# Seven block products instead of eight in one more tile of a hybrid block's output projection, with the weights' sums made by accumulating DMAs

## The reference

```
h     = rmsnorm(x, w_norm_pre)
proj  = h @ w_in                      # 1024 -> 3328 columns: q_a k_a v_a z_a q_r f_r i_r z_r
o_a   = sliding_window_attention(rope(q_a), rope(k_a), v_a, sinks) * silu(z_a)
o_r   = rmsnorm(hgrn2(q_r, f_r, i_r)) * silu(z_r)
y     = concat([o_a, o_r]) @ w_out    # 1024 -> 1024
out   = x + rmsnorm(y, w_norm_post)
```

## Time and profile before

| | |
|---|---|
| median of 3 runs | 865.61 us (865.39 to 866.41) |
| the profiled execution, its own time | 864.57 us |
| its span in the trace | 862.7 us |
| granted TensorE clock, mean | 0.999 |
| TensorE busy | 851.9 us |
| VectorE, ACT, GpSimd busy | 631.9, 519.0, 114.6 us |
| moved by DMA | 211.20 MB, mean 245 GB/s |

### The profile page before, as it was taken

The page is one execution under the profiler, slowest core; times in us unless marked ns, Lnnn a source line. Parts: engine busy times, 40 slices in busy tenths (PEclk is TensorE's granted clock), DMA queues, the critical chain, the costliest instruction groups (busy, mean ns, idle before and its releaser), DMA issues.

```text
span 862.7 us, 12445 instructions
## 1 busy us (share of the span) xinstructions
PE 851.9 (99%) x4428; PEld 700.6 (81%) x4428; DVE 631.9 (73%) x1125; ACT 519.0 (60%) x1033; POOL 114.6 (13%) x84
## 2 busy tenths in 40 slices
PE   8999999999999999999999999999999999999997
PEld 6787788888888778888888878888888887888885
DVE  6878878674656799767747789887775368888846
ACT  7766445763466458567446655865853755576544
POOL 0000013430200000332020000144300000004220
PEclk9999999999999999999999999999999999999999
DMA  8686755748986647464898785445699674444586
GB/s 322 212 325 221 244 205 170 285 147 314 418 342 248 213 145 265 152 210 133 321 382 348 276 330 172 146 151 216 241 374 396 228 273 147 147 147 158 189 326 254
DMA packets 59981, 211.20 MB, mean 245 GB/s; under 512 B 6672, under 2 KB 6928, under 8 KB 59920
## 3 DMA queue, kind: packets, MB, share of 16 engines
q1 hardware_dynamic: 57904, 205.56, 65.3%
q10 hardware_dynamic: 2016, 4.85, 1.4%
HBM read 157.95 MB, written 52.43 MB: 244 GB/s over the span
## 4 chain that ended last, share of the span: by engine, by line
PE 84%; DVE 9%; ACT 4%; issue 3%; DVEq 0%
PE bank L596 55%; PE bank L605 5%; PE turn_b L852 3%; PE score_b L852 3%; PE bank L852 3%; PE score_b L605 3%; PE turn_b L605 3%; PE turn_b L653 2%; DVE kv_tok L1386 2%; PE score_b L629 2%; PE turn_b L706 2%; PE bank L697 1%; PE bank L687 1%; PE turn_b L709 1%; ACT probs_t L951 1%
## 5 line engine op out<-in xcount | busy, mean ns | idle before, releaser
L596 PE MATMUL bank<-h_hi,w_lo 128*128 128x512 f32 x832 | 326.9, 393 | 0.0
L596 PE MATMUL bank<-h_lo,w_hi 128*128 128x512 f32 x832 | 326.3, 392 | 0.0
L596 PE MATMUL bank<-h_hi,w_hi 128*128 128x512 f32 x832 | 324.4, 391 | 0.5 <-issue 0.5
L596 PEld LDWEIGHTS bank<-h_lo,w_hi 128*128 128x128 f32 x832 | 156.4, 188 | 34.7 <-issue 3.3
L596 PEld LDWEIGHTS bank<-h_hi,w_hi 128*128 128x128 f32 x832 | 156.4, 188 | 33.1 <-issue 1.0
L596 PEld LDWEIGHTS bank<-h_hi,w_lo 128*128 128x128 f32 x832 | 156.3, 188 | 32.8
L1716 POOL TENSOR_TENSOR mix_lo<-v_r,mix_hi 128x512 fp32r<-128x512 f32 x16 | 21.2, 1322 | 539.0 <-ACT v_r L1142 539.0
L1263 DVE TENSOR_TENSOR w_lo<-w_raw,w_hi 128x1024 fp32r<-128x1024 f32 x36 | 44.8, 1248 | 34.6 <-ACT w_hi L924 34.1
L1386 DVE STREAM_TRANSPOSE kv_tok<-k_mid 32x128 f32<-32x128 f32 x192 | 58.1, 303 | 2.8
L924 ACT ACTIVATE w_hi<-w_raw 128x1024 fp32r<-128x1024 f32 x38 | 39.8, 1051 | 24.9 <-issue 10.2
L1700 POOL TENSOR_TENSOR x_acc<-x_acc,x_sq 128x512 f32<-128x512 f32 x21 | 32.7, 1557 | 70.0 <-ACT x_sq L974 70.0
(11 more groups left out here) (280 smaller groups left out, 1549.2 us busy)
## 6 DMA issues: line engine op xcount, KB each, us to landing
w_hi<-kept_hi SPq DMA_DIRECT2D x108, 512.0 KB, 3.8
w_lo<-kept_lo SPq DMA_DIRECT2D x108, 512.0 KB, 4.9
w_raw<-in_weights SPq DMA_DIRECT2D x46, 512.0 KB, 6.2
kept_hi<-w_hi SPq DMA_DIRECT2D x34, 512.0 KB, 6.3
kept_lo<-w_lo SPq DMA_DIRECT2D x34, 512.0 KB, 7.4
x_in<-in_x_rows SPq DMA_DIRECT2D x8, 1024.0 KB, 8.1
x_in<-in_x SPq DMA_DIRECT2D x15, 512.0 KB, 6.6
kept_lo<-w_raw SPq DMA_DIRECT2D x8, 512.0 KB, 7.0
```

Of the source, the lines that this page charges most:

```text
L596: mm = pe.matmul(acc(w)[:, :], stationary[:, s, k, :], moving[:, k, :], start=(m == 0), stop=(m == 3 * KT - 1), skip_group_check=True)
```

## The change

FAST goes from 2 to 1: tile 1's output projection takes the form of seven block products too. LATE goes from 6 to 2: in tile 1 only weight tiles 0 and 1 are loaded raw and split; 2 to 5 are loaded from the kept parts, which are saved four positions earlier in tile 0 than before.

The sums of weight blocks are no longer made by VectorE. GpSimd issues eight DMAs of 1 MiB in tile 0, from the seventh split on: a block is copied in DRAM to `t_rows`, and another is added to it by an accumulating DMA. There are six phases with a wait between them. The signs of two sums turn, so VectorE negates in `sum_head` and `post`. SP loads the eight sums (512 KiB each): two at tile 0's weight tile 26, two at the start of tile 1 (into the attention's buffers `probs` and `probs_t`), four at its weight tile 4 (into `w_raw`). ACT and VectorE split them in tile 1's steps 1 to 5 (`sum_high`, `sum_low`; the high parts go to `mix_hi` and `mix_lo`), and SP saves them at tile 1's weight tiles 6, 7, 8, 9, 11, 13, 15 and 17. VectorE's first softmax of tile 1 waits until those in the attention's buffers are saved (`probs_saved`).

```diff
+LATE = 2
-FAST = 2
+FAST = 1
-SUMS_IN = (FAST - 1, H0 + 8), (FAST, 5)
-SUMS_OUT = ((FAST, 0, 0), (FAST, 1, 2)), ((FAST, H0, 0), (FAST, H0 + 2, 2))
-SUMS_AT = 5
+SUMS_IN = {(FAST - 1, OUT0): (0, 1), (FAST, 0): (2, 3), (FAST, LATE + 2): (4, 5, 6, 7)}
+SUMS_SPLIT = {1: (0,), 2: (1, 2), 3: (3, 4), 4: (5, 6), 5: (7,)}
+SUMS_OUT = {6: 0, 7: 1, 8: 2, 9: 3, 11: 4, 13: 5, 15: 6, 17: 7}
-LATE = 6
...
+            def load_sum(k):
+                if k == 0:
+                    sp.wait_ge(t_made, 64)
+                if k == 2:
+                    sp.wait_ge(weighed.sem, weighed.after(FAST - 1, PAIRS - 1))
+                    sp.wait_ge(head_mixed.sem, head_mixed.after(FAST - 1, HEADS - 1))
+                if k >= 4:
+                    sp.wait_ge(lo_split.sem, lo_split.after(0, 0) + FRESH - RAW_SLOTS + k - 4)
+                sp.dma_start(t_in[k], t_rows[k * P:(k + 1) * P, :].rearrange("p (k m) -> p k m", k=KT)).then_inc(t_loaded[k], 16)
+            def save_sum(k):
+                sp.wait_ge(t_low, k + 1)
+                rows, saved = slice((WT + k) * P, (WT + k + 1) * P), probs_saved if k in (2, 3) else t_saved
+                sp.dma_start(kept[0][rows, :].rearrange("p (k m) -> p k m", k=2), t_hi[k].bitcast(FP32)).then_inc(saved, 16)
+                sp.dma_start(kept[1][rows, :].rearrange("p (k m) -> p k m", k=KT), t_in[k]).then_inc(saved, 16)
...
-                    if i == FRESH + 1:
-                        for late in range(FRESH + 1 - RAW_SLOTS, FRESH):
-                            save_split(late)
+                    if i == FRESH:
+                        save_split(FRESH - 3)
+                    for k in SUMS_IN.get((t, w), ()):
+                        load_sum(k)
                     if i >= FRESH:
                         load_split(t, w)
+                    if i == FRESH + 1:
+                        for late in (FRESH - 2, FRESH - 1):
+                            save_split(late)
+                    if t == FAST and w in SUMS_OUT:
+                        save_sum(SUMS_OUT[w])
...
+            def sum_high(k):
+                act.wait_ge(t_loaded[k], 16)
+                act.activation(t_hi[k], t_in[k].rearrange("p k m -> p (k m)").rearrange("p (k n) -> p k n", k=2), ACT.Copy).then_inc(t_high, 1)
...
+                            if t == FAST and head == 0:
+                                act.wait_ge(probs_saved, 64)
                             act.activation(o_sq_hi, out_b, ACT.Square)
...
                 dve.wait_ge(turned.sem, turned.after(t, q - 1))
+                if t == FAST and q == 0:
+                    dve.wait_ge(probs_saved, 64)
...
-                dve.tensor_tensor(s_tmp[:, S2, :], h_mix[:, 2 * P:], s3[:, h, :], ALU.subtract).then_inc(s_step, 1)
+                dve.scalar_tensor_tensor(s_tmp[:, S2, :], h_mix[:, 2 * P:], -1.0, s3[:, h, :], ALU.mult, ALU.subtract).then_inc(s_step, 1)
...
+            def sum_low(k):
+                dve.wait_ge(t_high, k + 1)
+                dve.tensor_tensor(t_in[k], t_in[k], t_hi[k].rearrange("p k n -> p (k n)").rearrange("p (k m) -> p k m", m=P), ALU.subtract).then_inc(t_low, 1)
...
-            pool.wait_ge(lo_split.sem, lo_split.after(0, 3))
+            pool.wait_ge(lo_split.sem, lo_split.after(0, 6))
+            def sum_start(dst, src):
+                pool.dma_start(t_rows[dst * 2 * P:(dst + 1) * 2 * P, :], src).then_inc(t_base, 16)
+            def sum_add(dst, src):
+                pool.dma_start(t_rows[dst * 2 * P:(dst + 1) * 2 * P, :], src, accum_op=ALU.add, max_dma_last_dim=4 * KT * P).then_inc(t_made, 16)
+            def block_rows(w):
+                return weights[w * P:(w + 2) * P, :]
+            sum_start(0, block_rows(B11))
+            sum_start(1, block_rows(B22))
+            pool.wait_ge(t_base, 32)
+            sum_add(0, block_rows(B12))
+            sum_add(1, block_rows(B12))
+            pool.wait_ge(t_made, 32)
+            sum_start(2, t_rows[2 * P:4 * P, :])
+            pool.wait_ge(t_base, 48)
+            sum_add(2, block_rows(B11))
+            pool.wait_ge(t_made, 48)
+            sum_start(3, t_rows[4 * P:6 * P, :])
+            pool.wait_ge(t_base, 64)
+            sum_add(3, block_rows(B21))
```

More of the change, by code:

```diff
@@ L68 @@
 FAST_WT = OUT0 + len(FAST_ROWS)
-SPLIT_SLOT += [w % 4 for w in range(WT)] + [(WT + w) % 4 for w in range(FAST_WT)] * (TILES - FAST)
-assert WT == 34 and OUT0 == 26 and FAST_WT % 4 == 0 and FAST == 2
+SPLIT_SLOT += [w % 4 for w in range(FAST_WT)] * (TILES - FAST)
+assert WT == 34 and OUT0 == 26 and FAST_WT % 4 == 0 and FAST == 1
 UNITS = [(w, k, i) for w, ks in ((P1A, (0, 1)), (P1B, (2, 3)), (P7A, (0, 1)), (P7B, (2, 3)), (P2A, (0, 1)), (P6A, (0, 1)), (P4A, (0, 1)))
@@ L187, in after, with hybrid_block @@
         return self.per_tile + (sum(self.sizes[:tile]) if tile >= 0 else tile * self.per_tile) + i + 1
-def hybrid_block(nc, x, x_rows, weights, cos, sin, vectors, w_post, squares, out, kept):
+def hybrid_block(nc, x, x_rows, weights, cos, sin, vectors, w_post, squares, out, kept, t_rows):
     ctx = ExitStack()
@@ L270, in hybrid_block @@
         u4 = [probs[:, 4 * i:4 * i + 4, :].rearrange("p b n -> p (b n)") for i in range(2)]
-        t_hi = [t_more[:, 0, :, :], t_probs[:, 1, :, :], t_more[:, 1, :, :], t_probs[:, 0, :, :]], \
-               [mix[:, 2 * i:2 * i + 2, :] for mix in (mix_hi, mix_lo) for i in range(2)]
+        t_in = [area[:, i, :, :] for area, n in ((t_more, 2), (t_probs, 2), (w_raw, RAW_SLOTS)) for i in range(n)]
+        t_hi = [mix[:, 2 * i:2 * i + 2, :] for i in (2, 3, 1, 0) for mix in (mix_hi, mix_lo)]
         y_stats = sb("y_stats", [16])
@@ L343, in hybrid_block @@
         a_sum, y_kept, y_took, y_posted = (Count(sem(n), i, 0) for n, i in (("a_sum", 1), ("y_kept", 6), ("y_took", 8), ("y_posted", 8)))
[L344 removed]
+        t_base, t_made, t_high, t_low, t_saved = (sem(n) for n in ("t_base", "t_made", "t_high", "t_low", "t_saved"))
+        t_loaded = [sem(f"t_loaded{i}") for i in range(T_TILES)]
+        probs_saved = sem("probs_saved")
         lo_split = count("lo_split", WT)
@@ L1650, in _ @@
                             sum_head(t, h)
-                    if t == FAST and 0 <= s - SUMS_AT < 4:
-                        sum_weights(1, s - SUMS_AT)
-                    for i in splits(t, s) if (t, s) != (1, 0) and (t or kind not in (0, 1)) else ():
+                    for k in SUMS_SPLIT.get(s, ()) if t == FAST else ():
+                        sum_low(k)
+                    for i in splits(t, s) if t or kind not in (0, 1) else ():
                         if i in DVE_LOW:
@@ L1660, in _ @@
                         dve.tensor_scalar(y_bias[:, :], y_sq[:, 0:4], 1.0 / D_MODEL, EPS, ALU.mult, ALU.add).then_inc(y_biased.sem, 1)
-                        for part in range(4) if t == FAST - 1 else ():
-                            sum_weights(0, part)
                 if t >= FAST:
@@ L1670, in _ @@
                         dve.tensor_tensor(mix_lo[:, 0, :], x_acc[:, :], mix_hi[:, 0, :], ALU.subtract).then_inc(x_low, 1)
-                    if b == 3 and t == 0:
-                        for i in splits(1, 0):
-                            split_lo(i)
                     copy_y(t, 1, b)
```

72 lines of the change are left out of this document (18 added, 54 removed).

## The result

The change made the kernel slower: 876.01 us (median of 4 runs, 874.72 to 876.92) against 865.50 beside it, a ratio of 1.0118 (95%: 1.0106 to 1.0130). I had forecast 861.6. The profiled execution took 874.72 us; its span is 872.9, where before's is 862.7.

A forecast was written before the change was run, and what follows sets the result against it. TensorE bounds the kernel, busy 851.9 of 862.7 us. -4.6 + 0.1 + 0.4 + 0.1 = -4.0 us on the profiled 864.57 gives 860.6; with the runs' median 1.04 above, 861.6, range 860.0 to 864.6.

The forecast's parts named there:

- the order at the change of tiles: SP's transfers from tile 0 to 1: 14.5 MiB behind 217.6 take 36.3 us, with 36.5 us to spend.
- The term "0.4": TensorE's wait at tile 1's weight 5 (load 39): 0.4 us, taken between 0 and 1.8.
- tile 0 at nothing: Tile 0: five phases of accumulating DMAs take about 50 us, four more saves fit in; nothing reaches TensorE.
- Rival 4: Tile 0: slow accumulates make GpSimd late; at 124 us TensorE loses 28 us, total 889; chance 0.04.
- the form's gain: Tile 1's output projection: 24 fewer matmuls, 5.44 us, pay 4.38 us net.
- the 0.2: Tile 2: VectorE's sums of weights leave it, which gives about 0.2 us back.
- rival 2: Change of tiles: queue runs at 390 to 400 GB/s, wait 1.8 to 2.5 us, total 863.0 to 863.7; chance 0.16.
- rival 3: Change of tiles: queue can't hold 2 MiB a step, rate falls to 355 GB/s, total 868.9; chance 0.05.
- Split 34: First weight of tile 1: low part done at 226.3, wanted at 226.45, cover gone; put at 0.1 us.
- VectorE's wait for the saved sums: Tile 1's first softmax: saves end about 273.9, buffer written at 274.01; a microsecond late is covered.
- ACT's lateness: Tile 1's rotated queries: about 3.0 us later, up to 0.9 more, cover 1.1; costed at nothing, 0.1 in the sum.
- rival 1: Tile 1: ACT's lateness reaches the scores, 1.3 us more, total 862.9; chance 0.10.

The follow-up runs named there:

- Experiment 2: Changed kernel without GpSimd's eight accumulating and copying DMAs, plain weight blocks loaded in place of the sums: 871.05 us, ratio 1.0056 to before.
- Experiment 1: Changed kernel with load 38 (weight 4 of tile 1) issued ahead of the four last sums' loads: 872.26 us, ratio 1.0064 to before.
- Experiment 5: Experiment 1 plus saves 34 and 35 issued ahead of loads 36 and 37 (weights 2 and 3 of tile 1): 867.01 us, ratio 1.0018 to before.
- experiments 1 to 5: Experiment 1, Experiment 2, experiment 4, Experiment 5, and the changed kernel with the edits of Experiment 1 and Experiment 2 together: 867.39 us, ratio 1.0017.
- 7: Changed kernel with the edits of Experiment 5 and 6 together, everything computed, run twice: 862.59 and 862.86 us, ratios 0.9975 and 0.9973 to before.
- experiment 9: 7 with the last four sums loaded a weight or two later in pairs, splits stretched to step 7, saves moved behind: 865.18 us, ratio 0.9996.
- 6: Changed kernel with GpSimd's chain begun at the fourteenth split, last three phases between GpSimd's own operations: 871.73 us, ratio 1.0078 to before.
- Experiment 8: Changed kernel with the sums neither made, loaded, split nor saved, plain blocks streamed in their place: 861.40 us, ratio 0.9958 to before.
- experiment 4: Changed kernel with the four accumulating DMAs made plain DRAM to DRAM copies, additions left out: 873.97 us, ratio 1.0085 to before.

## Why the prediction was wrong

**The step that failed first: the order at the change of tiles.** I carried the queue forward as bytes behind 217.6, put the last four sums behind load 38, and let load 36 go as soon as TensorE was done with tile 0. I had load 38's wait for save 34, but not load 36's wait for save 33, and the code puts the sums ahead of load 38. Experiment 2, in which tile 0 loses nothing, shows this at the prediction's own times (its chain, then two windows of 4 us):

```profile
228.75 0.32 SPq L472
...
231.77 12.23 DMA kept_lo<-w_lo
...
244.43 11.57 DMA w_lo<-kept_lo
...
228.00:232.00 4.00, 4.00 (x20) 3.29 (x19) 3.76 (x6) 3.64 (x14) 3.22 (x3) 1.00 0.50 148
232.00:236.00 4.00, 4.00 (x19) 3.34 (x18) 3.90 (x5) 0.72 (x2) 2.51 (x2) 1.00 0.98 287
```

Load 36 is issued at 228.75 (forecast 226.7). Save 34 lands at 244.0 (forecast 237 to 239). Load 38 lands at 256.0 (forecast 246.4), where TensorE wants it at 248.7 as forecast. The term "0.4" measured 7.3 us and some 2 more at the lower clock. Carried forward with the two facts, the rate of 2.5 us a MiB would have shown a part of it, by an estimate: loads 36 to 38, saves 34 and 35, the four sums and ACT's stores are 9 MiB behind 228.7, done at 251.2, a wait of 2.5 us. Most of the rest, by the same kind of estimate, is the queue that ran down while SP stood at load 36: 148 and 287 GB/s in the two windows, where 414 to 417 are moved from 240 to 256. Experiments 1 and 5 undo the two, one after the other: the wait goes from 7.3 to 4.0 to 0.7 us. The sign I had named for it came, a wait on the kept rows of over 2 us at weights 4 to 6; the DMA share of 1.0 through to 270 that I expected is broken at 232.

**The second: tile 0 at nothing.** I forecast 50 us for the accumulates' five phases and got 62.3, which alone is harmless as I said: GpSimd still idled 35 us. But I priced them only by GpSimd's wait and never by what they do to the ring beside them. And I priced the four saves by the share of one slice. The two together cost 4.5 us, by way of a save that lands 26 us after its issue, ACT's next split and the softmax behind it. Rival 4 had the right suspect with the wrong victim: its price of 28 us was GpSimd's lateness, which didn't happen.

**What was right.** Most of the form's gain: the kernel with no sums takes 3.6 us off the time, and its tile 1 is 3.7 us shorter with 0.4 us of waiting in it, so the form gives 4.1 where I took 4.4. In the kernels whose order is mended tile 1 takes 210.35 to 210.66, where before it was 213.53: 2.9 to 3.2 less, with 0.7 to 1.1 us of waits beside it, 3.9 to 4.0 in all. The term was 0.3 to 0.5 too large. Tile 2 gave 0.16 of the 0.2. The rate held at 393 to 420 GB/s, and at 410 or more from 244 on, so rivals 2 and 3 fall as rates. Split 34, for whose lateness I put 0.1, was waited for 0.2 to 0.5 us in experiments 1 to 5. The Trainium skill's page "DMA: Bandwidth & Descriptors", section "Where 436 GB/s comes from", puts one core's limit against HBM near 358 GB/s; the windows above, of a kernel on one core, disagree with it. VectorE's wait for the saved sums and ACT's lateness cost nothing in the changed kernel, nor in 5 and 7; something like rival 1 came once, when experiment 9 put low parts ahead of the first softmax.

**What closes the account.** After's span is 10.2 us above before's: 5.3 in tile 0 (0.2 of it at the start), 5.0 in tile 1, and 0.1 less behind. The 5.0 are 7.3 + 2 less the form's 4.1, which gives 5.2. Of the 5.07 us that tile 0 loses behind the scores, 2.7 are the two waits, some 1.7 the clock (0.86 and 0.71 in two windows of 4 us, an estimate), and 0.57 is there without the chain. Undoing the two gives 867.01 (5 alone), 871.73 (6 alone) and 862.6 to 862.9 (7): 9.0 and 4.3 of 876.01, and 13.2 to 13.4 together. That is 1.0 to 1.3 us above the forecast. Experiment 8 leaves about as much to the sums' remaining transfers: 0.7 is waits of TensorE in tile 1 (1.1 against 0.4), and 0.4 to 0.6 lie ahead of tile 1, of which only up to 0.3 is seen as a wait. The form gave less and the sums cost more than I had put; 8, which has no sums at all, is the one that reaches the forecast.

Still open: why the chain's cost needs a backlog of just this length. That the save lands 26 us after its issue against a cover of about 22 us (26 less ACT's wait of 4.35) is worked out from one execution. A run with two of the four saves would test it; it was not made.

## What to carry to other kernels

Carry a queue forward as a program, not as bytes: for every transfer write down each semaphore that holds it, above all those on earlier *saves* from the same buffer, and what stands behind it in its engine's order. A save put behind a load that waits for a save makes a relay; issuing the saves first was worth some 5 us here for a move of three lines. And where two things each use up the same cover, run them together before you call either free: the chain and the four saves each cost nothing that could be told, and 4.5 us together.

## What the runs showed of the hardware

- A second queue stretches the first. With GpSimd's transfers in flight beside SP's ring, SP's landings go from 6.3 to 7.4 us (experiment 2) to 17 to 23 us, and with plain copies in place of the accumulates they are still 17.6 to 20.1 (experiment 4).
- Accumulates fill the engines with fewer bytes. While they are in flight the DMA share is full (1.05 to 1.08 in the windows of 52 to 64 us) and only 267 to 280 GB/s are counted; with copies in the same phases 413 to 431 are, at a share of 1.01 to 1.03 (58 to 78 us of experiment 4).
- An accumulate of 1 MiB, DRAM to DRAM, beside the ring: GpSimd waited 19.4 us for the pair and 11.9 for a single one; for copies in the same places 11.0 and 9.0 (experiment 4). The software queue's share over the span is still only 3.6%.
- Around the 7.3 us without a matmul (253.93 to 261.27) TensorE's clock was granted at 0.83 in 256 to 260, 0.50 in 260 to 264, the 1.2 GHz level, and 0.82 in 264 to 268; around the 1.9 us wait in tile 0 it was 0.86 in 68 to 72 and 0.71 in 72 to 76. These two waits cost more than their length.
